# Dilated and neighbourhood attention by pairs of heads on the two row halves of the array, their bias added on VectorE, GpSimd's weight halves held back during VectorE's turns, and one conditioning product beside a chunk

## The reference

```
logits = einsum(q, k) * dh**-0.5 + bias[distance bucket, head]      # masked where out of the span
alpha  = softmax over the groups of their log denominators
o      = sum(alpha * group output)
```

```
s_win = einsum(q, k) * scale + rpb[row difference, column difference]   # masked outside 16 columns
p     = softmax(concat[s_win, q @ k_ctx * scale])
o     = p_win @ v + p_ctx @ v_ctx
```

## Time and profile before

| | us |
|---|---|
| three timed runs | 4033.42, 4050.34 (median), 4109.35 |
| the profiled execution, its own time | 4068.32 |
| its span from first to last instruction | 4066.7 |
| granted clock, mean over the span | 0.853 of full |

### The profile page before, as it was taken

How to read it: one execution, slowest core, us unless ns; L and a number is a source line. 1 busy time by engine, 2 the same in 40 slices (tenths; PEclk the granted TensorE clock), 3 DMA queues, 4 the chain that set the end, 5 groups by cost and what they waited for, 6 DMA issues and landing times.

```text
span 4066.7 us, 36201 instructions
## 1 busy us (share of the span) xinstructions
PE 3087.6 (76%) x13325; PEld 1936.9 (48%) x13325; DVE 1439.2 (35%) x2560; ACT 781.2 (19%) x1005; POOL 1009.7 (25%) x461
## 2 busy tenths in 40 slices
PE   4869689988697597698984777776396895777775
PEld 2657456666575375466664222222274664222221
DVE  2642433323423523723235222222626234222223
ACT  0323222213132111321110111111013220111111
POOL 0157345511476132201220000000244051000000
PEclk8989889989798798657996899998697596899997
DMA  7235358852353322001221999999222052999997
GB/s 270 70 124 171 128 206 285 285 124 32 101 176 119 110 73 80 13 8 65 83 73 46 329 374 377 371 374 357 94 94 74 28 178 88 362 373 372 376 374 268
DMA packets 362110, 763.36 MB, mean 188 GB/s; under 512 B 15044, under 2 KB 16242, under 8 KB 361216
## 3 DMA queue, kind: packets, MB, share of 16 engines
q1 hardware_dynamic: 337312, 669.61, 47.3%
q0 software_dynamic: 24672, 92.05, 7.6%
HBM read 716.28 MB, written 45.32 MB: 187 GB/s over the span
## 4 chain that ended last, share of the span: by engine, by line
PE 56%; DMA 24%; DVE 15%; issue 3%; ACT 1%; POOL 1%; SPq 0%; DVEq 0%; POOLq 0%; ACTq 0%
PE banks L644 10%; DMA weight_ring<-in_moe_w_up 10%; PE banks L645 10%; PE banks L649 9%; DMA weight_ring<-in_moe_w_down 5%; PE banks L874 4%; PE banks L788 4%; PE banks L670 4%; PE banks L896 4%; DMA weight_ring<-in_moe_w_gate 4%; PE banks L801 3%; PE banks L790 3%; PE banks L815 2%; DMA weight_ring<-in_dil_w_qkv 1%; PE banks L732 1%
## 5 line engine op out<-in xcount | busy, mean ns | idle before, releaser
L1307 POOL TENSOR_TENSOR weight_ring_r<-weight_ring,weights_high_r 128x2048 fp32r<-128x2048 f32 x124 | 567.5, 4583 | 865.8 <-ACT weights_high_r L1101 865.5
L874 PE MATMUL banks<-weight_ring,arena 128*64 128x512 f32 x2048 | 525.8, 640 | 213.3 <-DMA weight_ring<-in_moe_w_up 144.0
L644 PE MATMUL banks<-weights_high_r,x_transposed_r 128*128 128x512 f32 x1216 | 500.7, 412 | 94.9 <-DVE x_transposed_r L1519 27.4
L1101 ACT ACTIVATE weights_high_r<-weight_ring 128x2048 fp32r<-128x2048 f32 x124 | 234.1, 1897 | 875.3 <-PE banks L649 659.5
L649 PE MATMUL banks<-weight_ring_r,x_transposed_r 128*128 128x512 f32 x1600 | 390.0, 390 | 3.1 <-POOL weight_ring_r L1307 3.0
L874 PEld LDWEIGHTS banks<-weight_ring,arena 128*64 128x64 f32 x2048 | 133.3, 140 | 534.4 <-issue 208.3
L649 PEld LDWEIGHTS banks<-weight_ring_r,x_transposed_r 128*128 128x128 f32 x1600 | 299.5, 188 | 68.7 <-POOL weight_ring_r L1307 6.6
L1307 POOL TENSOR_TENSOR weight_ring_r<-weight_ring,gates_r 128x2048 fp32r<-128x2048 f32 (+1 forms) x60 | 273.1, 4564 | 187.6 <-ACT gates_r L1101 187.1
L732 PE MATMUL banks<-constants,scaled_rows 128*128 128x128 f32 x594 | 107.4, 343 | 273.4 <-DVE scaled_rows L1529 197.9
L644 PEld LDWEIGHTS banks<-weights_high_r,x_transposed_r 128*128 128x128 f32 x1216 | 239.7, 197 | 155.8 <-DVE x_transposed_r L1519 28.6
L1408 POOL DMA_DIRECT2D moe_y<-arena x64 | 34.0, 531 | 1085.3 <-DVE arena L1915 1067.6
(11 more groups left out here) (280 smaller groups left out, 4205.0 us busy)
## 6 DMA issues: line engine op xcount, KB each, us to landing
weight_ring<-in_moe_w_gate SPq DMA_DIRECT2D x128, 1024.0 KB, 10.4
weight_ring<-in_moe_w_up SPq DMA_DIRECT2D x128, 1024.0 KB, 8.7
weight_ring<-in_moe_w_down SPq DMA_DIRECT2D x128, 1024.0 KB, 10.6
weight_ring<-in_w_in SPq DMA_DIRECT2D x56, 1024.0 KB, 5.2
weight_ring<-in_w_ada SPq DMA_DIRECT2D x48, 1024.0 KB, 7.0
weight_ring<-in_ffn_w_in SPq DMA_DIRECT2D x44, 1024.0 KB, 5.1
weight_ring<-in_dil_w_qkv SPq DMA_DIRECT2D x36, 1024.0 KB, 5.2
weight_ring<-in_ffn_w_out SPq DMA_DIRECT2D x20, 1024.0 KB, 5.1
```

The lines of the kernel that those rows point to most:

```text
L644: nc.tensor.matmul(banks[t][:, 0:width], xh, wh[:, k, :], start=k0 + k == 0, stop=False)
L874: last = nc.tensor.matmul(halves(ps[m], kt), x, w[:, k, :], start=kt < 2, stop=kt >= KD - 2)
L1101: nc.scalar.activation(high(s, kn, width), slot(c, kn, width), ACT.Copy).then_inc(high_ready, 1)
L1307: nc.gpsimd.tensor_tensor(slot(c, kn, width, ring_r), slot(c, kn, width), high(s, kn, width), ALU.subtract).then_inc(low_ready, 1)
```

## The change

Five things change together.

1. **Dilated attention** by pairs of heads (`dilated` on each engine, 8 pairs). A score product is issued for both heads of the pair, one on rows 0 to 63 and one on rows 64 to 127. The bias product is gone: VectorE adds the bias to the scores and takes the extremum in one instruction that writes the biased scores to SBUF, and ACT takes the exponential from there. Signs are turned round (q scaled by -0.125, bias negated, minimum for maximum, exponential with scale -1). Transposes go to fixed banks, split in a left part of up to four blocks and a right part of two, with the copies shared between ACT and VectorE.
2. **Neighbourhood attention** in the same way (`neighbourhood`, 4 pairs by 2 or 4 tiles, one 512-column score product per head and latent tile instead of 2 of 256). POOL masks the bias tiles. The bias tiles are no longer reversed: two transfers on POOL's queue, issued during the latent attention, write each bias row 128 or 64 times one after the other to device memory (`skew_dram`, 48 x 128 x 384 values; `rpb_skew`, 240 x 64 x 127 values), so that a load with a row step one shorter than the row gives the tile as needed.
3. **GpSimd held back.** VectorE signals `port_free` at the end of a turn, and POOL waits for it (`after_turn`) before the low parts of the product that follows: three times in each `close_block`, before `g_dil`, before the first gate product and before `g_out` of each layer. The low parts of `g_kv` chunk 0 wait for the end of the norm turn (`x_ready`), those of the first gate product move behind the attentions.
4. **One conditioning piece a chunk**: 18 pieces beside `g_dil`, 4 beside `g_kv` and 2 beside `g_qz` of layer 0. The gate rows are transposed and stored at the start of each layer, and loaded for all partitions after the neighbourhood attention, ahead of the reload of the low activations and of the row `da_subln_g` on the same queue.
5. **Differential attention**: one reduction over both maps, one combining instruction instead of two (the scaling of L1614 is gone), and PE runs the previous unit's v product before the transposes.

```diff
         pieces = [(g_ada[i], n) for i in range(DEPTH) for n in range(ADA_N)]
-        ada_after, at = [], 0
-        for n in range(len(g_dil.chunks)):
-            more = 1 + (n % 3 == 2)
-            ada_after.append(pieces[at:at + more])
-            at += more
+        n_dil = len(g_dil.chunks)
+        side = {g_dil: pieces[:n_dil], g_kv[0]: pieces[n_dil:n_dil + 4], g_qz[0]: pieces[n_dil + 4:]}
+
+        def with_side(g):
+            out = []
+            for n in range(len(g.chunks)):
+                out.append((g, n))
+                out += side.get(g, [])[n:n + 1]
+            return out
...
+                def behind(n):
+                    if after is not None:
+                        after(n, done[n])
+                    if n < len(side.get(g, [])):
+                        pe.wait_ge(acc_used, ada_done[0])
+                        ada_done.pop(0)
+                        transposes([ada_row(g, n)[:, j * P:(j + 1) * P] for j in range(4)])
                 for n in range(len(g.chunks)):
                     product_chunk(g, n, lhs)
-                    if after is not None and n > 0:
-                        after(n - 1, made.now(acc_ready) - g.tiles)
-                if after is not None:
-                    after(len(g.chunks) - 1, made.now(acc_ready))
+                    done.append(made.now(acc_ready))
+                    if n > 0:
+                        behind(n - 1)
+                    if n < len(side.get(g, [])):
+                        ada_piece(side[g][n][0])
+                        ada_done.append(made.now(acc_ready))
...
+                def scores(j, t, groups=(0, 1, 2)):
+
+                    if j > 0:
+                        pe.wait_ge(dil_max, 4 * (j - 1) + (2 if t else 4))
+                    n = (t + 1) * P
+                    for g in groups:
+                        for m in range(2):
+                            last = nc.tensor.matmul(dil_scores_place(t, m)[:, g * n:(g + 1) * n],
+                                                    dqT[64 * m:64 * m + 64, g, j, t * P:(t + 1) * P],
+                                                    dkT[64 * m:64 * m + 64, g, j, 0:n], start=True, stop=True)
+                    if groups[-1] == DIL_G - 1:
+                        last.then_inc(dil_scores, 1)
...
+                scores(0, 1)
+                scores(0, 0)
+                for j in range(N_PAIRS):
+                    more = j + 1 < N_PAIRS
+                    turn_left(j, 0)
+                    if j > 0:
+                        values(j - 1, 3)
+                    if more:
+                        scores(j + 1, 1, (0, 1))
+                    turn_right(j, 0)
+                    if more:
+                        scores(j + 1, 1, (2,))
+                    turn_left(j, 1)
+                    turn_right(j, 1)
+                    if more:
+                        scores(j + 1, 0)
+                    turn_left(j, 2)
+                    values(j, 0)
+                    turn_left(j, 3)
+                    values(j, 1)
+                    values(j, 2)
+                values(N_PAIRS - 1, 3)
...
+                        done = na_max if steps[n - 2][1] < LT else na_exp
+                        pe.wait_ge(done, 2 * (base + n - 2) + 2)
+                    for m in range(2):
+                        last = nc.tensor.matmul(ps[n % 2 * 2 + m][:, 0:nk * P],
+                                                qcT[64 * m:64 * m + 64, j, t * P:(t + 1) * P],
+                                                kcT[64 * m:64 * m + 64, j, k0 * P:(k0 + nk) * P], start=True, stop=True)
+                    last.then_inc(na_scores, 1)
...
+                def exps(j, i):
+                    act.wait_ge(dil_max, 4 * j + i + 1)
+                    probs, c = dil_probs(j, i), dil_stat(j, i)
+                    nc.scalar.activation(probs, probs, ACT.Exp, bias=small[:, 64 + c:65 + c], scale=-1.0,
+                                         accum_out=small[:, 80 + c:81 + c]).then_inc(dil_exp, 1)
...
+            def after_turn():
+
+                pool.wait_ge(port_free, seen.next(port_free))
+
             def close_block(i, g_o):
+                after_turn()
                 low_parts(g_o)
                 row(I["norm_g"][i, 3])
                 load(ar(PLE, 512).rearrange("p (k t) -> p k t", k=2), I["p_t"][i].rearrange("(k p) t -> p k t", p=P))
+                after_turn()
                 low_parts(g_ff_in[i])
                 low_parts(g_ff_out[i])
                 if i == 0:
                     row(I["norm_g"][1, 1])
+                after_turn()
                 low_parts(g_ple_g[i])
...
+            nc.gpsimd.dma_start(skew_dram.rearrange("r (q m) -> r q m", m=BIAS_LEN),
+                                rel_dram.unsqueeze(1).broadcast_to([DIL_G * DIL_H, P, BIAS_LEN])).then_inc(skew_out, 16)
+            nc.gpsimd.dma_start(rpb_skew.rearrange("r (q m) -> r q m", m=RPB_W),
+                                rpb_dram.rearrange("l r w -> (l r) w").unsqueeze(1).broadcast_to(
+                                    [DEPTH * NA_H * RPB_R, GRID_W, RPB_W])).then_inc(rpb_out, 16)
             row(I["norm_g"][0, 1])
             close_block(0, g_mla_o)
+
+            def load_bias(j):
+                for m in range(2):
+                    src = bass.AP(tensor=skew_dram.tensor, offset=(2 * j + m) * P * BIAS_LEN + P - 1,
+                                  ap=[[BIAS_LEN - 1, P], [DIL_H * P * BIAS_LEN, DIL_G], [1, 2 * P]])
+                    nc.gpsimd.dma_start(dil_bias(j)[:, m], src).then_inc(bias_in[j % 2], 16)
+            pool.wait_ge(skew_out, 16)
+            load_bias(0)
+            after_turn()
             low_parts(g_dil)
-            for h in range(DIL_H):
...
+            pool.wait_ge(misc_ask, seen.next(misc_ask))
+            load_bias(1)
+            for j in range(2, N_PAIRS):
+                pool.wait_ge(dil_max, 4 * (j - 1))
+                load_bias(j)
...
                 row(I["da_lambda_2"][layer].rearrange("a b -> (a b)"), 256)
-                low_parts(g_kv[layer], [0])
                 pool.wait_ge(x_ready, layer + 1)
                 nc.gpsimd.dma_start(low_dram, Y_r[:, :]).then_inc(low_saved, 16)
+                low_parts(g_kv[layer], [0])
+                pool.wait_ge(misc_ask, seen.next(misc_ask))
+                nc.gpsimd.dma_start(gate_dram[layer].rearrange("(r c) -> r c", c=P),
+                                    gate_rows[0:4 * KD, layer * P:(layer + 1) * P]).then_inc(scratch_out, 16)
                 low_parts(g_kv[layer], [1, 2, 3])
+                pool.wait_ge(rpb_out, 16)
+                biased = [n for n, (j, t) in enumerate(na_steps(layer)) if t < LT]
...
+                def mask_bias(k):
+                    pool.wait_ge(na_bias_in[k % 4], 64 * (layer * 2 + k // 4 + 1))
+                    for m in range(2):
+                        b = na_bias(k, m)[:, 0:SEQ].rearrange("p (r c) -> p r c", r=4)
+                        ins = nc.gpsimd.tensor_tensor(b, C[:, C_NAMASK:C_NAMASK + GRID_W].unsqueeze(1).broadcast_to(
+                            [P, 4, GRID_W]), b, ALU.subtract)
+                    ins.then_inc(na_bias_ready, 1)
...
+                for k in range(4, len(biased)):
+                    pool.wait_ge(na_max, 2 * (base + biased[k - 4]) + 2)
+                    load_bias(k)
+                    mask_bias(k)
+                pool.wait_ge(na_out, base + len(na_steps(layer)))
+                pool.wait_ge(scratch_out, 16 * (DEPTH + DIL_G + layer + 1))
+                nc.gpsimd.dma_start(GT[:, :], gate_dram[layer].partition_broadcast(P)).then_inc(gates_in, 16)
                 nc.gpsimd.dma_start(A_r[:, XL:XL + KD * MAX_TILES * P], low_dram).then_inc(low_back, 16)
                 row(I["da_subln_g_2"][layer], P)
+                after_turn()
+                low_parts(g_gate[layer][0])
                 low_parts(g_gate[layer][1])
                 load(ar(ROUTER, 36 * KD).rearrange("p (k n) -> p k n", k=KD), I["router_w"][layer].rearrange("(k p) n -> p k n", p=P))
                 load(vrow[:, 0:36], I["router_b"][layer].partition_broadcast(P))
                 for n in range(2, 6):
                     low_parts(g_gate[layer][n])
+                after_turn()
                 low_parts(g_out[layer])
...
+                    if unit.kind == "diff":
+                        c = 64 + stat(units, u)
+                        v(red(small[:, c:c + 2], unit.scores.rearrange("p (m k) -> p m k", m=2)[:, :, 0:unit.n_keys], X,
+                              ALU.max, negate=True), max_ready)
+                        return
...
-                             ALU.mult))
-                        v(stt(unit.probs[:, 0:n], unit.probs[:, 0:n], small[:, c:c + 1],
-                              unit.probs[:, BANK:BANK + n], ALU.mult, ALU.add), p_ready)
+                        v(nc.vector.reciprocal(small[:, c + 1:c + 2], small[:, c + 1:c + 2]))
+                        v(stt(small[:, c + 1:c + 2], small[:, c + 1:c + 2], small[:, 96:97], small[:, c:c + 1],
```

(25 more changed lines are left out.)

517 lines of the change are left out of this document (327 added, 190 removed).

## The result

| | median us | runs |
|---|---|---|
| before | 4067.1 | 4033 to 4109, four |
| changed | 3723.9 | 3719 to 3729, four |

A forecast was written before the change was run, and what follows sets the result against it. TensorE was taken to bound the kernel where it has work, VectorE in the turns between products, slowed by GpSimd. The terms summed to -327 us: 3741 profiled, 3723 at the median, range 3640 to 3850.

The forecast's parts named there:

- dilated attention: Dilated attention: 168.7 us before, 86 us after, at 9.4 us a pair of heads plus head, tail and half-clock start; -82.
- six pieces in kv and qz: Layer 0's kv and qz products: six conditioning pieces moved beside them at 1.98 us each, nothing hiding them; +12, bounds 8 and 20.
- neighbourhood attention: Neighbourhood attentions at 2.4 GHz: layer 0 64 us for 136, layer 1 48 for 91; -115.
- differential attention: Differential attention, both layers: the L1614 scaling and one of two reductions go, TensorE waiting for part; -10, bounds 0 and -16.
- GpSimd held: Turns, layer starts and after gating units: VectorE no longer slowed, 109 us back, late first low parts cost 8; -101.
- lambda row: Both layers: lambda row no longer behind the 2 MB gates load, half of VectorE's wait comes back; -8.
- da_subln row, low activations: After neighbourhood attention: 2 MB gates load ahead of both on the queue, 8.3 us in each layer; +16, bounds 0 and 20.
- copies to device memory: Two repeating copies from the latent attention's start take 56 us, ahead of a norm row wanted at about 210; no cost.
- The likeliest case: Whole kernel: the forecast sum of -327, 3723 us at the median; chance 0.60.
- rival A: New dilated and neighbourhood attentions: TensorE stays at 1.2 GHz, +145, 3868 us; chance 0.11.
- rival D: GpSimd hold: only moves the stall to first low parts and VectorE's other losses, +30, 3753 us; chance 0.08.
- Rival E: Dilated and neighbourhood attentions: row halves don't overlap in long runs, 49 us, 3772 us; chance 0.06.

## Why the prediction was right, and where it was not

| step | forecast | measured, and where |
|---|---|---|
| dilated attention | -82 | -85: 168.5 to 83.0 |
| dilated product | -42 | -46: 310.4 to 264.5 |
| six pieces in kv and qz | +12 | +13: 220.0 to 233.5 |
| neighbourhood attention | -115 | -139: 135.7 to 53.4, 91.0 to 34.5 |
| differential attention | -10 | -27: 66.5 to 49.1, 39.8 to 30.0 |
| GpSimd held | -101 | -103 (run without the hold) |
| lambda row | -8 | -10: waits 9.6 and 8.1 to 3.8 and 3.9 |
| da_subln row, low activations | +16 | +9: stretch to the next product 25.8 to 30.1, 18.1 to 23.1 |
| copies to device memory | 0 | +46: the turn at 219, 37.5 to 68.5 with 15 of hold in it |
| gate transposes, small issues | +3 | no run measures it |

The measured rows add up to -342, and the profiled executions differ by 349. The row of the hold comes from another pair of kernels than the others.

**The likeliest case held in kind.** TensorE's list set the attentions, so durations of single products from one time line, multiplied, gave a pair as 9.4 us (8.9 measured) and a step as 4.1 (4.0). VectorE and ACT, at 40 and 41 of 84 us in the dilated attention, had the room that the added bias work needed. How much the missing bias products bring in the new lists is not measured by itself: no run puts them back. The clock rose, and rival A did not come: the new lists, with eight transposes in every step and 18 in every pair, ran at 0.92 to 1.00. The rule beside it, that a transpose doesn't count as busy in the same way (the Trainium skill, "TensorE: Matmul & The Clock Gate", Part 4: PE-mode transpose), is not put to a test: the 18 transposes take about 2 of a pair's 8.9 us. What decides between the levels for lists with one half at work is still open; both were seen. So the forecast of the clock came true, but its reason (two halves at work and no idle time between) is likely and not proved: the kernel before reached 2.4 GHz with one head at a time too.

**The hold.** The term was read instruction by instruction from the turns, and both runs with it alone bear it out. Of its two parts the price in late first low parts (8) was too high; rival D is out.

**What failed.** The step "At the rate of the 12.3 MB that landed in 40.2 us they take 56: nothing" took the rate of a store in rows of 1024 values for one in pieces of 508 B. That copy ran at 90 KB/us, not 306, and the norm row behind it came 45.8 us late. The ground for doubt was there, the rule and the lack of a row; I gave it 0.12. It was a bound that I should have laid into the sum.

**What was mis-sized.** Neighbourhood attention: the steps were right (51 and 33 us for 53.4 and 34.5 measured in all), the 13 us of head, tail and half clock that I added in each layer were not there. The clock was up already (0.90 in the differential attention ahead, 1.00 from the first step), and head and tail took 2.4 us at most. Differential attention: I priced VectorE's shorter lists and passed over the order of TensorE's list, which the same diff changes: 8.5 us in the stretches, 13 in the medians. The load of the gates was counted in full, where over half of the wait for the row belonged to the low activations ahead of it.

**Rival E** was priced at 25 for the dilated attention; the run with the halves apart shows 12. **Rival C** (slow bias loads) did not come: the skewed loads of 384 KB landed in 4 us. Its 14 x 24 is 336 and not 327; nothing hangs on that.

## What to carry to other kernels

Where one engine is full, its time line multiplied out is a forecast of a stretch to a few per cent, if the clock is known; what it leaves out are transfers of a kind that the trace does not yet show, and those need both ends of their price in the sum. Before a diff is costed, look at each engine's order as well as its instructions. Where a copy's rows can be padded from 508 to 512 B, pad them, spread weight loads evenly over a stretch that moves near the rate of the queues, and hold an engine that blocks VectorE's turns when it has nothing urgent to make.

## What the runs showed of the hardware

- Score products on rows 0 to 63 and 64 to 127 overlap even when four records of one half stand before those of the other in the list: eight of 256 columns in 1.07 us in either order.
- TensorE's clock can stay at 1.2 GHz for a whole attention in which it is busy without a break (halves apart: 158 of 161 us busy, granted clock 0.52). Other executions of the same list took 3730 to 3741 for its 3795, so they were likely at 2.4; none of them has a trace. With both halves at work the clock was at 2.4 for at least five sixths of the dilated attention in every profile (0.92 to 0.98); in the changed kernel it was up at the start, down from 812 to 825 and up again.
- GpSimd issued the second repeating copy only when the first had landed (issues at 137.3 and 171.7, landing at 171.2), and made nothing in the 32.3 us between. Size alone does not do that: the store of 12.3 MB and the one of 4.1 MB behind it were issued 1.5 us apart (16.9 and 18.4 in the kernel before). What makes the difference is open.
- A copy within device memory in rows of 508 B moved 90 KB/us, the same in rows of 512 B 204, one in rows of 1536 B 272.
